# Recurrent stage of a two-block layer kernel: decay rows spread by DMA, their exponents on GpSimd during the projection, two units started per slot pair, no barrier at entry

## The reference, cut to what matters

```python
gc = jnp.cumsum(chunks(g[..., None])[..., 0], axis=-1)     # log decay, summed in the chunk
dd = gc[..., :, None] - gc[..., None, :]
gam = jnp.where(tri, jnp.exp(jnp.where(tri, dd, 0.0)), 0.0)
a_kk = jnp.where(strict, jnp.einsum('bhnic,bhnjc->bhnij', kb, kc) * gam, 0.0)
sol = lax.linalg.triangular_solve(a_kk + eye, rhs, ...)
a_qk = jnp.einsum('bhnic,bhnjc->bhnij', qc, kc) * gam
def step(state, inp):
    v_new = un - jnp.einsum('bhck,bhkv->bhcv', wn, state)
    o = einsum(qn * exp(gn), state) + einsum(aqk, v_new)
    state = state * exp(g_last) + einsum(kn * exp(g_last - gn), v_new)
```

## Time and profile before

| | |
|---|---|
| median of the runs | 1965.51 us |
| profiled execution, own time | 1968.18 us |
| its span | 1966.4 us |
| busy in the span: PE, DVE, ACT, POOL | 1878.5, 817.7, 782.1, 597.8 us |
| gdn on PE, first to last start of L1032 | 184.0 to 416.5 us |
| PE's first matmul of zgate | 422.1 us |

### The profile page before, as it was taken

One profiled execution on the slowest core, in us unless ns is written; L12 is line 12 of the kernel. 1 busy time (PEld: TensorE's weight loads), 2 busy tenths in 40 slices (PEclk: granted clock), 3 DMA queues, 4 the chain that ended last, 5 costly groups with the idle time before them and its releaser, 6 DMA issues.

```text
span 1966.4 us, 23067 instructions
## 1 busy us (share of the span) xinstructions
PE 1878.5 (96%) x9756; PEld 1489.7 (76%) x9756; DVE 817.7 (42%) x1338; ACT 782.1 (40%) x1286; POOL 597.8 (30%) x182
## 2 busy tenths in 40 slices
PE   8998899989999999999899999989998999998997
PEld 5777799988788888887788888877674468765456
DVE  7663545653123212102562035135635644625653
ACT  5974465443333333223332122224335533334541
POOL 3331432032232333444254434433420005322001
PEclk9998899989999999999899999989999999999999
DMA  5110000122323332232132323223110012211001
GB/s 198 65 65 0 1 1 21 45 91 75 135 96 107 97 112 85 87 107 86 45 127 86 107 86 107 86 86 137 67 65 22 1 43 99 86 63 44 1 1 43
DMA packets 28992, 141.54 MB, mean 72 GB/s; under 512 B 2871, under 2 KB 7351, under 8 KB 14936
## 3 DMA queue, kind: packets, MB, share of 16 engines
q1 hardware_dynamic: 18944, 122.94, 17.4%
q10 hardware_dynamic: 9944, 17.12, 2.6%
HBM read 134.80 MB, written 5.24 MB: 71 GB/s over the span
## 4 chain that ended last, share of the span: by engine, by line
PE 90%; DVE 4%; ACT 3%; POOL 2%; issue 1%; DMA 0%; POOLq 0%; SPq 0%; DVEq 0%; ACTq 0%
PE bank L403 54%; PE bank L1032 8%; PE bank L607 5%; PE bank L414 4%; PE bank L1977 3%; PE bank L1998 3%; PE bank L1984 2%; PE bank L1437 1%; ACT w_part L361 1%; PE bank L1413 1%; PE bank L655 1%; PE bank L1926 1%; PE bank L792 1%; ACT WK L2107 1%; PE bank L1068 1%
## 5 line engine op out<-in xcount | busy, mean ns | idle before, releaser
L403 PE MATMUL bank<-x_part,w_part 128*128 128x512 f32 x3264 | 764.8, 394 | 0.6 <-DVE x_part L571 0.6
L403 PEld LDWEIGHTS bank<-x_part,w_part 128*128 128x128 f32 x3264 | 614.6, 189 | 135.0 <-issue 6.1
L2424 POOL TENSOR_TENSOR w_part<-RAW,w_part 128x2048 fp32r<-128x2048 f32 (+1 forms) x90 | 402.9, 4480 | 819.4 <-ACT w_part L361 819.4
L2424 POOL TENSOR_TENSOR w_part<-WK,w_part 128x2048 fp32r<-128x2048 f32 (+1 forms) x30 | 125.1, 4169 | 376.7 <-ACT w_part L361 376.7
L361 ACT ACTIVATE w_part<-RAW 128x2048 fp32r<-128x2048 f32 (+1 forms) x90 | 166.5, 1851 | 175.7 <-PE bank L403 138.3
L403 PE MATMUL bank<-f_part,w_part 128*128 128x512 f32 x768 | 174.4, 389 | 0.0
L403 PEld LDWEIGHTS bank<-f_part,w_part 128*128 128x128 f32 x768 | 144.1, 188 | 29.9
L1032 PE MATMUL bank<-WK 128*128 128x128 f32 (+1 forms) x1056 | 125.0, 279 | 5.3 <-DVE WK L1265 3.7
L1032 PEld LDWEIGHTS bank<-WK 128*128 128x128 f32 (+1 forms) x1056 | 119.7, 194 | 7.6 <-DVE WK L1265 4.0
L1977 PE MATMUL bank<-WK 64*128 64x512 f32 (+3 forms) x256 | 81.7, 593 | 9.7 <-ACT STAT L2093 9.7
L903 DVE SCALAR_TENSOR_TENSOR WK<-bank,COL,WK 128x510 f32<-128x510 f32 (+1 forms) x96 | 71.6, 749 | 46.3 <-ACT WK L863 43.7
(11 more groups left out here) (281 smaller groups left out, 2392.8 us busy)
## 6 DMA issues: line engine op xcount, KB each, us to landing
RAW<-wts SPq DMA_DIRECT2D x84, 1024.0 KB, 4.8
WK<-wts SPq DMA_DIRECT2D x24, 1024.0 KB, 4.8
WK<-scratch ACTq DMA_DIRECT2D x16, 256.0 KB, 2.7
RAW<-wts SPq DMA_DIRECT2D x6, 512.0 KB, 3.4
WK<-wts SPq DMA_DIRECT2D x6, 512.0 KB, 3.5
scratch<-WK ACTq DMA_DIRECT2D x4, 768.0 KB, 3.3
WK<-xT SPq DMA_DIRECT2D x4, 512.0 KB, 5.8
WK<-xT ACTq DMA_DIRECT2D x1, 2048.0 KB, 12.7
```

Of the source, the lines that this page charges most:

```text
L403: mm = pe.eng.matmul(b[:, :], W[w][:, k, c:c + P], src[x][k], start=start and k == 0 and n == 0, stop=stop and k == kn - 1 and n == 2)
L2424: eng.tensor_tensor(low_part(i), raw_part(i), high_part(i).bitcast(F32), ALU.subtract).then_inc(w_split, 1)
```

## The change

- **Decay rows.** PE transposes the summed decays into 16 rows once, behind tile n = 9 (`turn_rows`); ACT copies them out (n = 10) and writes them to DRAM. `load_rows(u)` reads, for each direction, 4 rows of 128 values into all 128 partitions (256 KB, pieces of 512 bytes), on ACT's queue. `gr` and L1127 are gone; POOL adds the column (a second operation of 128x512) and then the mask, in `exponent(u)`.
- **First units.** For units 0 to 3 (`EARLY`) the rows are loaded at n = 14 and n = 20 and `exponent` runs on POOL right behind its last weight piece of the projection. Their phases 0 and 1 are gone from the slots, which begin with slot -1. Their first `u` no longer takes L1216 and L1218 on POOL but a `mix` on ACT, a transpose on PE and its copy on ACT.
- **START** = (-3, -3, -3, -3, 9, 9, 13, 13). The last slot is 38 where it was 45.
- **No barrier** at the entry on PE, ACT, DVE, POOL; single waits instead. `turn(5)` and `trans(5)` stand in slot 0, `trans(4)` behind tile 22.
- **Next stage's weights** are rounded on ACT in slots 30 and 34.
- **Homes** of the buffers are two tables, and the exponents of units 2 and 3 lie in the output area until `qm` moves them.

```diff
-        START = (0, 1, 2, 3, 12, 13, 19, 20)
+        EARLY = 4
+        START = (-3, -3, -3, -3, 9, 9, 13, 13)
...
+            def turn_rows():
+                b = job("rows")
+                pe.wait_ge(*at("gcc"))
+                for t in range(TT):
+                    mm = pe.eng.transpose(b[0:16, t * P:(t + 1) * P], GCUM[:, t, :], ident)
+                mm.then_inc(*pe.did(("pe", "rows")))
...
+                if n == 10:
+                    act.wait_ge(*at(("pe", "rows")))
+                    act.eng.activation(ROWT[0:16], ps("rows")[0:16, :], ACT.Copy).then_inc(*act.did(free="rows"))
+                    act.wait_ge(*act.last())
+                    act.eng.dma_start(rows, ROWT[0:16]).then_inc(rows_out, 16)
+                if n == 14:
+                    act.wait_ge(*at("rows_out"))
+                    load_rows(0)
+                    load_rows(1)
+                if n == 20:
+                    act.wait_ge(*at(("scaled", 3, 3)))
+                    load_rows(2)
+                    load_rows(3)
+                if n == 22:
+                    trans(4)
             finish(len(tiles) - 1)
-            trans(4)
-            trans(5)
...
+        def load_rows(u):
+
+            c, hf = units[u]
+            for d in range(2):
+                src = bass.AP(tensor=rows.tensor, offset=(8 * d + 4 * hf) * S + c * P, ap=[[0, P], [S, 4], [1, P]])
+                q["act"].eng.dma_start(gamma(u, d), src).then_inc(rows_in[u], 16)
...
-            for slot in range(last):
+            for slot in range(-1, last):
...
+                if slot == 0:
+                    yield "values", None, None, None
+                if slot in (30, 34):
+                    yield "weights", None, first_after_gdn + (slot - 30) // 4, None
...
-            pe.stage("gdn")
+            pe.stage("gdn", barrier=False)
...
-                elif ph == 3:
+                if ph == 3:
+                    if u == 0:
+                        pe.wait_ge(*at(("scaled", 3, 3)))
...
-                        elif l > 1:
+                        elif l > 1 or u < EARLY:
                             pe.wait_ge(*at(("mixed", u, l - 1)))
                             four(("ut", u, l - 1), lambda o, h: E.transpose(o, UC[:, h, :], ident))
...
-            for gi in range(4):
-                act.wait_ge(*at(("pe", ("ov", 2, gi))))
-            ahead(upto=first_after_gdn + 1)
+                    for gi in (2, 3) if a == first_after_gdn else (0, 1, 2, 3):
+                        act.wait_ge(*at(("pe", ("ov", int(a > first_after_gdn), gi))))
+                    ahead(upto=a)
...
+            def exponent(u):
+                c, hf = units[u]
+                pool.wait_ge(*at(("rows", u)))
+                for d in range(2):
+                    g, k = gamma(u, d), 8 * d + 4 * hf
+                    G.tensor_tensor(g, g, NEGC[:, c, k:k + 4].unsqueeze(2).broadcast_to([P, 4, P]), ALU.add).then_inc(*pool.did())
+                    pool.wait_ge(*pool.last())
+                    G.tensor_tensor(g, g, b4(dmask(d)), ALU.add).then_inc(*pool.did(("ddm", u, d)))
+
+            for u in range(EARLY):
+                exponent(u)
...
-                    G.tensor_tensor(UC, A, b4(pair_mask), ALU.mult).then_inc(*pool.did())
-                    pool.wait_ge(*pool.last())
-                    G.tensor_tensor(UC, b4(ident), UC, ALU.subtract).then_inc(*pool.did(("u", u, 0)))
+                    if u >= EARLY:
+                        G.tensor_tensor(UC, A, b4(pair_mask), ALU.mult).then_inc(*pool.did())
+                        pool.wait_ge(*pool.last())
+                        G.tensor_tensor(UC, b4(ident), UC, ALU.subtract).then_inc(*pool.did(("u", u, 0)))
```

More of the change, by code:

```diff
@@ L173, with build @@
 NTAB = 3840
[L176 removed]
+def build(nc, xT, cols, base, gdnc, tabs, wgate, relb, sel, small, wts, out, scratch, rows, old):
     subs = sub_list()
@@ L331, in build @@
         table["gdnc"] = (gdnc_in, 16)
+        table["rows_out"] = (rows_out, 16)
+        for u in range(8):
+            table[("rows", u)] = (rows_in[u], 32)
         table["wgate"] = (wgate_in, 16)
@@ L781, in dst_tile, with turn, trans @@
             return QF[:, 4 * c + i, :] if c < 2 else KF[:, 4 * (c - 2) + i, :] if c < 4 else SI[:, i, :]
+        def turn(c):
+            pe = q["pe"]
+            for i in range(4):
+                n = ("tr", c, i)
+                b = job(n)
+                pe.wait_ge(*at(("ktile", c, i) if c < 4 else ("vtile", c, i)))
+                for t in range(TT):
+                    mm = pe.eng.transpose(b[:, t * P:(t + 1) * P], dst_tile(c, i)[:, t * P:(t + 1) * P], ident)
+                mm.then_inc(*pe.did(("pe", n)))
+        def trans(c):
+            act = q["act"]
+            dst = KTOK if c < 4 else VTOK
+            for i in range(4):
+                act.wait_ge(*at(("pe", ("tr", c, i))))
+                act.eng.activation(dst[:, :, (c % 2) * 4 + i, :], ps(("tr", c, i))[:, :].rearrange("p (t c) -> p t c", c=P),
+                                   ACT.Copy).then_inc(*act.did(*([("tok", c)] if i == 3 else []), free=("tr", c, i)))
         def qkv_pe():
@@ L819, in qkv_pe @@
                         turn(4)
-            turn(5)
+                    if c == 2 and i == 1:
+                        turn_rows()
         def qkv_act():
@@ L1108, in gdn_pe @@
                     invert(a, ph)
-                else:
+                elif kind == "step":
                     step(a, b, ph)
+                elif kind == "values":
+                    turn(5)
         def gdn_act():
@@ L1114, in gdn_act, with mix @@
             A = act.eng
[L1115 removed]
+            act.stage("gdn", barrier=False)
+            act.wait_ge(*at("bk"))
+            act.wait_ge(*at("gdnc"))
+            def mix(u, l):
+                act.wait_ge(*at(("t", u, l)))
+                uc = uc_of(u).rearrange("p h c -> p (h c)").rearrange("p (m two b) -> p m two b", two=2, b=2 << l)
+                A.activation(uc, t_mixed(u, l + 1), ACT.Copy).then_inc(*act.did(("mixed", u, l)))
             def invert(u, ph):
[L1118 removed]
                 if ph == 0:
[L1120 to L1128 removed]
+                    load_rows(u)
                 elif ph == 2:
@@ L1202, in gdn_pool @@
                 if ph == 1:
-                    for d in range(2):
-                        pool.wait_ge(*at(("dd", u, d)))
-                        G.tensor_tensor(qm(u, d), qm(u, d), b4(dmask(d)), ALU.add).then_inc(*pool.did(("ddm", u, d)))
+                    exponent(u)
                 elif ph == 3:
```

94 lines of the change are left out of this document (48 added, 46 removed).

## The result

The changed kernel took 1935.49 us (median of 4 runs, 1932.14 to 1935.61), the kernel before 1965.29 beside it (4 runs, 1963.92 to 1968.25): a ratio of 0.9843, 95% interval [0.9826, 0.9859]. The forecast was 1932.5. The profiled execution took 1935.57 us with a span of 1933.8; against the profiled one of before (1968.18) that is 32.6 us less, where 33.0 was forecast.

A forecast was written before the change was run, and what follows sets the result against it. PE, busy 96% of the span, bounds the kernel; only less PE work, standing or low clock pays. Zgate 32.7 us earlier plus 1.2 less 0.9 gives 33.0 off 1968.18; less 2.67, 1932.5 us, range 1925 to 1942.

The forecast's parts named there:

- Rival A: Stage entry stays bound by its feeders, with late rows or larger slot waits: gain only 13 to 22 us; chance 0.14.
- The first of the two rules weighed: Projection: DVE's two-input SBUF reads can stall under POOL's operations; four L925 at most 1.3 us each, 5 us to spare.
- Entry: Stage start: level 1 `p` and the new transpose end at 198.9, bounds 195 to 206; worth 29.4 us if later loss stayed.
- Later loss: Stage behind the entry: PE's waits and half-speed stretches sum to 19.8 us, against 17.6 before; bounds 8 to 35.
- (a): Slots 9 to 12: POOL's exponents of units 4 and 5 delay ACT's exponents and copies; PE loses 3 us.
- (b): Slot 13: POOL does three operations for unit 4 before `t` of unit 5; PE waits 1.6 and 2.9, 4.5 us.
- (c): Slot 17: units 6 and 7 wait on POOL as units 4 and 5 do in slot 13; 2.3 us.
- (d): Tail of the steps: DVE, 3.9 us per step, follows PE, 4.5; costs 3 us.
- (e): Half-speed PE stretches behind the entry and behind (b), 3.5 us each; 7 us.
- Rival D: Waits in every slot keep PE at 1.2 GHz for much of the stage: slower than before, to 2010; chance 0.05.
- Exit: Stage end: PE ends at 389.4 and zgate starts at once instead of at 422.1, 32.7 us; full clock 1.2 more.
- rival C: Stage end: zgate's weights not ready, PE waits about 5.5 us again; gain 26, 1940; chance 0.10.

The follow-up runs named there:

- e3: Changed kernel, but ACT rounds zgate's first two weight pieces behind the last step again, as before: 1936.06 us, 0.9844 of the kernel before.
- e1: Changed kernel with an entry barrier on GpSimd alone, so the early exponents come after the projection: 1949.69 us, 0.9900 of the kernel before.
- e8: Changed kernel with units 5 and 7 starting one slot later than 4 and 6: 1926.25 us, 0.9795 of the kernel before.
- the changed kernel again: The changed kernel itself, unedited, run on another chip: 1932.19 us, 0.9826 of the kernel before.
- e5: Changed kernel with the decay rows of units 4 to 7 all fetched in slot 2: 1933.56 us, 0.9834 of the kernel before.
- e6: Changed kernel with ACT's mix for all units, two POOL operations of units 4 to 7 gone: 1926.60 us, 0.9791; again on another chip 1925.03, 0.9793.
- e7: Changed kernel with the edits of e5 and e6 together: 1928.17 us, 0.9805 of the kernel before.
- e11: e6 with the rows of units 4, 5, 6, 7 fetched in slots 2, 4, 6, 8: 1920.14 us, 0.9764 of the kernel before.
- e2: Changed kernel with the entry barrier on TensorE, ScalarE and VectorE, none on GpSimd: 1928.04 us, 0.9799 of the kernel before.
- e12: e11 with the entry barrier on TensorE, ScalarE and VectorE, none on GpSimd: 1916.56 us, 0.9752 of the kernel before.

## Why the prediction was right, step by step

**Projection.** Forecast 0.9 us longer, measured 1.7 (177.2 against 175.5), 0.44 of it `turn_rows`. The rest is a stretch at the lower clock: PEclk 0.93 between 60 and 84 us, where before had 1.00, and where the e3 kernel, with the same projection, was granted 1.00 and began the stage at 175.9.

**Early exponents.** Forecast 20.3 us under the projection, done by 172; they took 19.4, from 143.07 to 174.8, since L1255 takes 1.04 us where I had 1.27. POOL, its instructions (start, us):

```profile
143.07 1.06 POOL L1255 TENSOR_TENSOR WK<-WK,STAT 128x512 f32<-128x512 f32 x1
...
165.32 1.04 POOL L1255 TENSOR_TENSOR WK<-WK,STAT 128x512 f32<-128x512 f32 x1 [11.94 <-DMA WK<-decay_rows]
```

The rows of unit 2 were asked for at 159.29, 3 us later than the forecast's 156, and came 6 us behind that, within its 3 to 7; the last operation ended 7 us before the first exponent (181.89). Rival A needed them 20 us late. e1 shows what the cover was worth: 15.5. The first of the two rules weighed could be seen here and cost nothing: under POOL's operations DVE's four L954 (L925 in before) took 4.70 us from 149.83, where four take 2.7 alone, the longest 1.78; PE did not wait.

**Entry.** Slot 3 was forecast for 198.9, or 199.8 with the 0.9 of the projection, and PE's unbroken work begins at 200.76: the silu's end was 1.9 late, and each step behind it came in its place (exponents with the table load 1.28, `decay` at 184.48, DVE's twelve operations to 193.1, POOL's `t` from 193.77). The rule that speaks against the change, that waits bring the low clock with them, did not bite in this execution: PE stood for 5.5 us of 16.3 and was granted 1.00. That was luck. Over 181.5 to 200.8 only this execution and that of e8 were granted 1.00; the changed kernel again and e3, e5, e6 (both executions), e7 and e11, with the same entry, were granted 0.91. The rows, first of after, then of the changed kernel again:

```profile
193.49:201.64 8.15, 6.86 (x61) 6.62 (x60) 4.76 (x8) 4.78 (x8) 5.01 (x4) 1.00 0.01 2
...
192.95:201.12 8.17, 6.88 (x47) 6.64 (x46) 4.03 (x7) 4.35 (x7) 4.98 (x4) 0.79 0.01 2
```

The second execution did 47 records there in place of 61. In e11 PE did as many as in after over 181.5 to 200.8 (109) at 0.91: its slow stretch lay over transposes behind which PE would have waited. One step was sized rightly and valued wrongly: the early `kk` and `qk` fill time that PE would otherwise stand later (e2).

**Later loss.** Forecast 19.8, measured 17.5: 188.2 us from slot 3 (200.8) to zgate (389.0) less 170.7 of work. The row 200.80:389.20 splits it: 188.40 - 177.67 = 10.7 of standing, and the low clock is the other 6.8. Term by term: (a) 3 forecast, 2.7 measured, by the chain described, except that the row loads, not only POOL, stretched it (5.07 of the 15 us); (b) 4.5 against 1.7 + 2.6; (c) 2.3 against 2.1; (d) 3 against 1.5; together 10.6, which is the standing of the row; (e) 7 against 6.8. In (e) the sum was right and the places were not: the forecast had half of it behind the entry and half behind (b); here it lay behind (a), (b) and (c), with nothing at the entry, while the second execution was slow at the entry and not behind (c). e6 and e11 show the causes of (a), of (c) and of the wait of 2.6 in (b) by taking them away; the 1.7 of (b) stays in both. The rows are those of after behind (b) and (c), then that of the changed kernel again behind (c):

```profile
258.66:266.81 8.15, 4.47 (x23) 4.28 (x24) 1.64 (x3) 0.19 (x1) 7.99 (x7) 0.66 0.47 118
...
291.25:299.39 8.14, 6.03 (x39) 5.83 (x38) 2.76 (x4) 1.38 (x3) 5.02 (x5) 0.79 0.00 0
...
291.02:299.20 8.18, 6.06 (x54) 5.87 (x53) 3.91 (x6) 1.82 (x3) 6.98 (x6) 1.00 0.00 0
```

**The clock.** e11 also shows the price of a wait. Against the changed kernel PE stands 8.5 us less (7.8 against 16.3) and loses 5.1 less to the low clock (1.7 against 6.8), and the stage is 11.7 us shorter (376.3 - 176.2 against 389.0 - 177.2) though PE has 1.8 us of transposes more in it. So one us of wait in this stage costs about 1.6, an estimate from 13.5 over 8.5; the low clock of one kernel alone moved by 1.7 between two executions (e6), which is 0.2 of that figure. The Trainium skill (TensorE: Matmul & The Clock Gate, Part 1) has activity as what releases the full clock; here the trace agrees in kind. Rival D, in which the stage would stay at 1.2 GHz, was far off: 0.97 over the stage.

**Exit.** Forecast 389.4, or 390.3 with the 0.9 of the projection, measured 389.0: the entry 1.0 later and the later loss 2.3 less. There was no gap behind the last matmul; rival C (a gap of 5.5) didn't come, and e3 puts its price at 3.5. The third weight piece: ACT's rounding at 401.50 (forecast about 403), POOL's part done at 408.2 (near 409); PE did not wait for it.

**The sum.** 33.0 forecast against 32.6 between the two profiled executions. That they are so close is in part chance. zgate began 33.1 earlier where the sum has 31.8 (32.7 less 0.9). The 1.2 for the full clock at zgate's start came as 1.6: from zgate to the first matmul of dil it was 51.8 us before (422.1 to 473.9) and is 50.2 after (389.0 to 439.2). Behind that the changed kernel lost 2.1, of which the sum has no term. The forecast of the median (1932.5) is 3.0 below the measured 1935.49, by its last step: it took off 2.67 us because the profiled execution of before lay that much above its median, and that of after lay at its own. On the second chip the median was 1932.19. The mechanism was right; of the 3 us by which the medians on the two chips differ no step of the sum speaks.

## What the rest of the program adds

From zgate on, all variants execute the same instructions, and yet take 1537.3 to 1544.8 us in the profiled executions; with the low clock of that part subtracted (26.2 to 35.8 us by the same sum) it is 1509 to 1513 in all of them. In the traces this is made of stretches at the lower clock that lose about 1.7 us each; the runs of one kernel spread over some such stretches (1930.72, 1930.98, 1933.41, 1935.30), though only the second of these has a trace. Why some variants have fewer (e2, e6 again and e12: 26.2 to 26.6; the changed kernel 35.8 and 30.6) stays open; no run here was made for it. It bounds what can be said: e8 and e2 beat the changed kernel in the whole time without a place in the stage that explains it.

## What to carry to other kernels

Taking work from in front of a stage and putting it on an idle engine under the stage before is worth what the chain then waits for next, not what the work costs: 15.5 us for 18.7 here, and nothing for work of the engine that must wait for the same release anyway. Count a DMA issue as work of the engine that issues it, and spread issues over slots: eight in one slot cost 5 us of PE's time, two in each of four cost none. When changes of a few us are compared, compare a marker in the trace at the end of the changed stage beside the whole time, and in more than one execution: e6's marker moved by 3.2 us between two.

## What the runs showed of the hardware

A row load of 256 KB in pieces of 512 bytes landed after 3.5 to 8.8 us, median 7.0; a load of the same size by the page of before took 2.7. With the last eight of them spread over four slots (e11) their medians were 4.4 us into WK and 4.6 into RAW; with these eight in one slot (e5) 7.2 and 6.2. In that row of eight ACT's issues took 0.37 us for the first, 0.53 each for the next four, and 1.98, 1.81 and 1.46 for the last three.

GpSimd's add with a column of STAT broadcast as second operand took 1.04 us, the one with a mask repeated over the four heads (L1257) 1.29 and the one with two full operands (L1272) 1.28, all at 128x512.

VectorE and GpSimd slowed each other where both had two SBUF operands and overlapped. In after, a VectorE operation of 0.69 us took 5.00 under a GpSimd weight piece that had begun 0.6 us before it, and that piece 5.07 where the one at 138.52 took 4.60 (start, us; first VectorE, then GpSimd):

```profile
407.21 1.51 DVE L1437 TENSOR_TENSOR WK<-WK 128x512 f32<-128x512 f32 x1 [8.08 <-ACT WK L1414]
408.75 5.00 DVE L1440 TENSOR_TENSOR WK<-WK 128x512 f32<-128x512 f32 x1
...
414.39 0.69 DVE L1440 TENSOR_TENSOR WK<-WK 128x512 f32<-128x512 f32 x1
```

```profile
408.13 5.07 POOL L2492 TENSOR_TENSOR w_part<-WK,w_part 128x2048 fp32r<-128x2048 f32 x1
```

The Trainium skill (GPSIMD Engine Reference, Key points) names this contention; here it cost the path nothing: PE's waits between 389 and 480 are 0.2 us in all.
